# Reordering VectorE's work within a group of a Mamba-2 mixer, with finer waits

## The reference

```
proj = h @ w_in                      # z, x, B, C, dt
xBC  = silu(causal_conv4(xBC))       # depthwise, 4 taps
# 8 groups, each with its own B, C (128 states) and 4 heads of 64
a_cum = cumsum(dt * A) within a chunk of 128 positions
y_diag = ((C B^T) * exp(a_cum_q - a_cum_s), causal) @ (x dt)        # within a chunk
states = B^T (exp(a_end - a_cum) x dt), carried over the 4 chunks
y_off  = exp(a_cum) * (C @ carried state)                          # inter-chunk part
y = y_diag + y_off + x * d_skip
y = rmsnorm_per_group(y * silu(z)) * norm_g ;  out = y @ w_out
# samples: h_new = exp(dt A) h_old + dt B x^T ;  y = C h_new  (h: 8 x 32 x 64 x 128)
```

## Time and profile before

| | us |
|---|---|
| median of 3 runs | 1680.85 (1678.82 to 1683.0) |
| profiled execution | 1682.01 |
| its span, first to last instruction | 1680.3 |

### The profile page before, as it was taken

How to read it: one execution, slowest core, us unless ns; L and a number is a source line. 1 busy time by engine, 2 the same in 40 slices (tenths; PEclk the granted TensorE clock), 3 DMA queues, 4 the chain that set the end, 5 groups by cost and what they waited for, 6 DMA issues and landing times.

```text
span 1680.3 us, 30210 instructions
## 1 busy us (share of the span) xinstructions
PE 1571.3 (94%) x12653; PEld 1545.7 (92%) x12653; DVE 909.1 (54%) x1020; ACT 618.4 (37%) x827; POOL 374.0 (22%) x431
## 2 busy tenths in 40 slices
PE   6898878979987899999999999999999999999996
PEld 5898877879886799999999999999999999999996
DVE  3477688772876785343444453464455535344353
ACT  5656646622665242121212343342233212122221
POOL 1067576650665730000000022200001000000001
PEclk9999898989998999999999999999999999999998
DMA  5354445343544332332232332222223232233221
GB/s 151 93 158 127 138 129 164 118 133 94 147 125 136 107 104 81 96 101 91 85 100 76 101 114 89 76 77 89 89 76 101 76 101 89 89 99 98 78 76 51
DMA packets 158910, 173.19 MB, mean 103 GB/s; under 512 B 13912, under 2 KB 146896, under 8 KB 158784
## 3 DMA queue, kind: packets, MB, share of 16 engines
q1 hardware_dynamic: 137032, 131.30, 25.6%
q0 software_dynamic: 9472, 26.50, 5.6%
q10 hardware_dynamic: 12288, 13.71, 2.8%
HBM read 159.53 MB, written 12.21 MB: 102 GB/s over the span
## 4 chain that ended last, share of the span: by engine, by line
PE 63%; DVE 1%; ACT 1%; issue 0%; POOL 0%; ACTq 0%; DVEq 0%
PE ps L510 61%; PE ps L859 1%; PE ps L530 1%; PE ps L827 0%; PE ps L774 0%; PE ps L553 0%; DVE w_lo L1551 0%; PE ps L625 0%; POOL ssum L1415 0%; ACT arena L1359 0%; ACT w_hi L914 0%; PE ps L899 0%; PE ps L851 0%; POOL arena L1483 0%; DVE work L1557 0%
## 5 line engine op out<-in xcount | busy, mean ns | idle before, releaser
L510 PE MATMUL ps<-h_hi,w_hi 128*128 128x260 f32 (+2 forms) x2320 | 482.0, 289 | 5.2 <-issue 4.6
L510 PE MATMUL ps<-h_lo,w_hi 128*128 128x260 f32 (+2 forms) x2320 | 472.0, 285 | 0.0
L510 PE MATMUL ps<-h_hi,w_lo 128*128 128x260 f32 (+2 forms) x2320 | 471.9, 285 | 0.0
L1551 DVE TENSOR_TENSOR w_lo<-w,w_hi 128x2048 fp32r<-128x2048 f32 (+2 forms) x122 | 280.3, 2298 | 183.2 <-ACT w_hi L914 183.2
L510 PEld LDWEIGHTS ps<-h_hi,w_hi 128*128 128x128 f32 x2320 | 365.4, 192 | 7.8 <-issue 5.8
L510 PEld LDWEIGHTS ps<-h_lo,w_hi 128*128 128x128 f32 x2320 | 363.5, 191 | 0.0
L510 PEld LDWEIGHTS ps<-h_hi,w_lo 128*128 128x128 f32 x2320 | 363.2, 191 | 0.0
L914 ACT ACTIVATE w_hi<-w 128x2048 fp32r<-128x2048 f32 (+2 forms) x122 | 229.3, 1879 | 326.9 <-PE ps L510 326.7
L510 PE MATMUL ps<-a_hi,w_hi 128*128 128x260 f32 x1504 | 307.2, 286 | 9.2 <-DVE a_lo L1642 5.3
L510 PE MATMUL ps<-a_hi,w_lo 128*128 128x260 f32 x1504 | 305.5, 285 | 0.0
L510 PE MATMUL ps<-a_lo,w_hi 128*128 128x260 f32 x1504 | 305.0, 285 | 0.0
(11 more groups left out here) (208 smaller groups left out, 1370.4 us busy)
## 6 DMA issues: line engine op xcount, KB each, us to landing
w<-in_mlp_w_up SPq DMA_DIRECT2D x32, 1024.0 KB, 5.7
w<-in_mlp_w_down SPq DMA_DIRECT2D x32, 1024.0 KB, 5.2
w<-in_ssd_w_in SPq DMA_DIRECT2D x16, 1024.0 KB, 6.4
w<-in_cm_w_in SPq DMA_DIRECT2D x16, 1024.0 KB, 5.7
w<-in_ssd_w_in SPq DMA_DIRECT2D x16, 512.0 KB, 6.6
arena<-in_state_ssm POOLq DMA_DIRECT2D x64, 128.0 KB, 3.8
arena<-scr_a ACTq DMA_DIRECT2D x16, 512.0 KB, 3.9
arena<-scr_bc POOLq DMA_DIRECT2D x32, 256.0 KB, 3.9
```

Of the source, the lines that this page charges most:

```text
L510: mm = pe.matmul(ps[:, 2 * slot + b, 0:tn], w[:, pair.slot, k, col:col + P], x[:, k, t0:t0 + tn], start=(k == 0 and n == 0), stop=(k == ti ...
L1551: nc.vector.tensor_tensor(w_lo[:, pair.slot, k, w], w32[:, pair.slot, k, w], w_hi[:, pair.slot, k, w].bitcast(F32), ALU.subtract).then_inc ...
```

## The change

Nothing is computed otherwise; VectorE's list is reordered, three waits of other engines are bound to earlier marks, and the semaphore `cchain` now counts the decay products of the inter-chunk part only.

- `combine` is cut in two. The new `combine` does the product with the decay for both tiles and then adds it into `work` (new semaphore `yadd_done`). The new `gate` does the two 8-column sample operations (new `ysmp_done`), which wait for sample 3, and then the gate products.
- VectorE's order behind `y_diag(g,0)` and the first convolution becomes: `xdt` scaling, `y_diag(g,1)`, second convolution, `split_w`, sample 0, `states`, third convolution, sample 1, `combine`, fourth convolution, samples 2 and 3, `gate`.
- In window 7: `xdt` scaling, `y_diag(g,1)`, `evac_out(1)`, `split_w`, sample 0, `evac_out(2)`, `states`, sample 1, `evac_out(3)`, `combine`, samples 2 and 3, `gate`. Before, sample 0 stood ahead of `evac_out(0)` there.
- TensorE's `state_out` and the wait ahead of it ask for `cchain` in place of `comb_done`; ScalarE's `abc_load(g,0)` asks for `yadd_done`.

```diff
@@ -631,7 +633,7 @@
                 pe.wait_ge(hstep_done, 4 * g + 4)
-                pe.wait_ge(comb_done, 2 * g + 1)
+                pe.wait_ge(cchain, 2 * g + 1)
@@ -652,7 +654,7 @@
                 if due(2 * g - 1):
-                    pe.wait_ge(comb_done, 2 * g - 1)
+                    pe.wait_ge(cchain, 2 * g - 1)
@@ -1114,7 +1116,7 @@
                     if due(2 * g):
-                        act_e.wait_ge(comb_done, 2 * g)
+                        act_e.wait_ge(yadd_done, 2 * g)
@@ -1697,21 +1699,26 @@
             def combine(g):
 
                 for i in range(2):
-                    n = 3 * (2 * g + i)
                     dve.wait_ge(yoff_done, 2 * g + i + 1)
                     dve.wait_ge(ef_done, 2 * g + i + 1)
                     nc.vector.tensor_tensor(abc[:, 0, i, CH:TP], ps[:, 5 + i, CH:TP], abc[:, 0, i, CH:TP], ALU.mult)\
                       .then_inc(cchain, 1)
-                    if i == 0:
-                        dve.wait_ge(sred_done, 4 * g + 4)
+                for i in range(2):
+                    dve.wait_ge(cchain, 2 * g + i + 1)
+                    dve.wait_ge(y1_done, 2 * g + i + 1)
+                    nc.vector.tensor_tensor(work[:, i, CH:TP], work[:, i, CH:TP], abc[:, 0, i, CH:TP], ALU.add)\
+                      .then_inc(yadd_done, 1)
+
+            def gate(g):
+
+                dve.wait_ge(sred_done, 4 * g + 4)
+                for i in range(2):
                     nc.vector.scalar_tensor_tensor(out=work[:, i, TP:T], in0=act[:, g % 2, 2 + i, S0:CONV_N:TAPS],
                                                    scalar=dtf[:, 2 * g + i, 16:17], in1=ysmp[:, i, :],
-                                                   op0=ALU.mult, op1=ALU.add).then_inc(cchain, 1)
-                    dve.wait_ge(cchain, n + 1)
-                    dve.wait_ge(y1_done, 2 * g + i + 1)
-                    nc.vector.tensor_tensor(work[:, i, CH:TP], work[:, i, CH:TP], abc[:, 0, i, CH:TP], ALU.add)\
-                      .then_inc(cchain, 1)
-                    dve.wait_ge(cchain, n + 3)
+                                                   op0=ALU.mult, op1=ALU.add).then_inc(ysmp_done, 1)
+                for i in range(2):
+                    dve.wait_ge(ysmp_done, 2 * g + i + 1)
+                    dve.wait_ge(yadd_done, 2 * g + i + 1)
                     dve.wait_ge(evac_done, Pair(group_pair(g, 2)).unit(i, 1))
                     nc.vector.tensor_tensor(work[:, i, :], work[:, i, :], zs[:, i, :], ALU.mult)\
                       .then_inc(comb_done, 1)
@@ -1748,41 +1755,39 @@
                 split_w(Pair(group_pair(nxt, 1) if more else J_OUT1 + 1))
                 if not more:
                     y_low(g - 1)
-                    sample(g, 0)
-                if not more:
                     evac_out(0)
                 decayed(g, 1)
                 y_diag(g, 0)
                 if more:
                     conv(nxt, 0)
-                if not more:
-                    evac_out(1)
-                sample(g, 0 if more else 1)
-                split_w(Pair(group_pair(nxt, 1) + 1 if more else J_OUT1 + 2))
-                if more:
-                    conv(nxt, 1)
                 dve.wait_ge(ydiag_done, 2 * g + 2)
                 nc.vector.tensor_tensor(xdt[:, :, :].rearrange("p c (h d) -> p c h d", d=HD),
                                         xdt[:, :, :].rearrange("p c (h d) -> p c h d", d=HD),
                                         tokS[:, 1, :, 4 * g:4 * g + 4].unsqueeze(3).broadcast_to([P, NC, 4, HD]),
                                         ALU.mult).then_inc(xdte_done, 1)
                 y_diag(g, 1)
+                if more:
+                    conv(nxt, 1)
+                else:
+                    evac_out(1)
+                split_w(Pair(group_pair(nxt, 1) + 1 if more else J_OUT1 + 2))
+                sample(g, 0)
                 if not more:
                     evac_out(2)
-                if more:
-                    sample(g, 1)
-                if more:
-                    conv(nxt, 2)
                 if g == 0:
                     dve.wait_ge(cdec_landed, 16)
                 states(g)
-                sample(g, 2)
+                if more:
+                    conv(nxt, 2)
+                sample(g, 1)
                 if not more:
                     evac_out(3)
+                combine(g)
                 if more:
                     conv(nxt, 3)
+                sample(g, 2)
                 sample(g, 3)
-                combine(g)
+                gate(g)
 
 
             dve.wait_ge(par_landed, 48)
```

More of the change, by code:

```diff
@@ L337, in hybrid_step @@
         comb_done = sem("comb_done")
+        yadd_done = sem("yadd_done")
+        ysmp_done = sem("ysmp_done")
         ysq_done = sem("ysq_done")
```

## The result

The changed kernel took 1720.16 us (median of 4 runs, 1717.48 to 1723.23), the kernel before 1679.84 us beside it (4 runs, 1678.57 to 1683.0): the ratio is 1.0238, with a 95% interval of 1.0214 to 1.0261. It is slower by 40 us, where 17 were forecast. The direction was right and the time lies above the range.

The account below looks back on a forecast made before the run. The prediction took a ring through GpSimd, without TensorE, as the bound. Five regular groups +2.5, group 0 +3.1, group 3 +1.4 and group 7 +9.0 gave 16.0 us more than 1682.01: 1698, set at 1697 for the median; range 1673 to 1711.

Parts of the forecast that it names:

- The ring through GpSimd: Per-group cycle from VectorE's last gate through ScalarE, first convolution, GpSimd's states, sample 3 and combine: 59.08 us in group 2.
- C: In each group, the moment the next group's first convolution ends on VectorE; 26.94 us after the gate in group 2.
- the landing of the third state: GpSimd's third-state load in a regular group: predicted to arrive at C+14.1 against C+11.6 before, 2.5 us later.
- the upper bound of C+15.8: Latest predicted third-state landing in a regular group: C+7.7, 2.0 us of issuing, then 6.1 us of waiting.
- turns between queues: Rival for the third-state load: GpSimd waits 6 us again after a load issued 4.2 us later; 1711 us; chance 0.14.
- the predicted +3.1: Group 0's term: state landing +7.0 us, states 2 and 3 -1.9, gate -2.0; together +3.1.
- its ring was 58.2 and would be like the others, 59.6: Group 3's term, whose load had no weights beside it (3.29 us) but C came 2.5 us late: +1.4 us.
- the ring point: Where VectorE's last gate ends and the next group's split starts; 59.08 us apart across group 2.
- Five regular groups: Groups 1, 2, 4, 5 and 6: landing +2.5 and shorter combine -2.0 us give +0.5 each, +2.5 in all.
- Group 7: Last group's term: third-state landing +12.9 us, states 2 and 3 -1.9, gate -2.0; together +9.0.
- The cut of `combine`: Less VectorE work behind the last sample: the 384-column products and additions leave the ring, 2.0 us in each of 8 groups.
- The upper bound of the sum (+30): Sum with the latest landing: five times +2.2, group 0 +4.9, group 3 +3.1, group 7 +10.8 us; 1711 us.

Follow-up runs that it names:

- experiment 3: Kernel before with only combine cut in two, the gate alone last and the finer waits; sample, scaling and convolution order as before: 1668.21 us, ratio 0.9933.
- experiment 9: Kernel before with one edit on GpSimd: after each state, loads for the next are issued ahead of this one's stores: 1654.96 us, ratio 0.9841.
- experiment 1: Changed kernel with only sample 0 put back behind the first convolution, in group 7 ahead of evac_out(0): 1661.12 us, ratio 0.9891.
- experiment 2: Kernel before with only sample 0 moved late, behind xdt scaling and y_diag(g,1) (in window 7 sample 1 stays behind it): 1713.07 us, ratio 1.02.
- experiment 4: Changed kernel, with SyncE issuing a group's middle weights only once GpSimd has taken up the third state: 1696.77 us, ratio 1.0106.
- 7: experiment 6's kernel with sample 1 earlier still, ahead of the state steps, and GpSimd's loads ahead of its stores: 1651.15 us, ratio 0.9837.
- experiment 8: experiment 6's kernel with GpSimd's loads ahead of its stores and nothing else: 1650.61 us, ratio 0.9806.
- experiment 10: Changed kernel with GpSimd's loads ahead of its stores and nothing else: 1702.86 us, ratio 1.0134.
- experiment 6: experiment 1's kernel with sample 1 also a place forward, between the state steps and the third convolution: 1658.06 us, ratio 0.9872.
- experiment 5: Changed kernel with sample 0's product one place forward, just ahead of the split of the middle weights: 1685.57 us, ratio 1.0035.

## Why the prediction was right or wrong

**Right: what bounds the kernel.** The ring through GpSimd sets the time and TensorE is not in it. Two edits that leave TensorE's wait for scaling in place gained 12 us (experiment 3) and 25 us (experiment 9), and the change that removed both of TensorE's waits lost 40. What was said of the parts beside the ring held: the waits at L706 and L636 went, and TensorE's wait moved to the transposes behind SiLU, 12.8 us each where about 10 were given.

**Right: where the moved sample bites.** GpSimd resumes at C+7.7, as summed; it waits 3.73 us there (about 4 predicted) and 11.19 in group 7 (12 predicted); from sample 3 to the split 2.95 us (3.0). Putting the sample back takes the whole loss away (experiment 1), and moving it alone makes most of it (experiment 2).

**Wrong: the landing of the third state.** The step was: "In between: the weights wait for the split, are now issued at C+7.1 ... so C+14.1. I take it since the same transfers compete, with the weights further ahead." Measured: C+16.1, a little above even the upper bound of C+15.8. The step that failed is the price of the overlap: it added the 6.99 us which had passed between the issue of the weights and the landing to a later issue of the weights. But in the kernel before half of the state load was already out when the weights were issued, and now none of it is: from the weights' issue (238.81) to the state (248.05) it is 9.24 us. The wait after the issue was 6.42 us in this group and 5.9 to 6.9 in seven of eight, as it had been where weights came in among the load (6.13). With the weights held back it was 2.5 to 4.5 (experiment 4), with the weights 5.0 us ahead 2.99 (experiment 2), with them 4.8 us behind the first issue 2.95 (experiment 1). The head start of 0.8 us was too short to be worth anything. The rival "turns between queues" described this; it had a chance of 0.14 and its 1711 was also too low.

"The same transfers compete" left out ScalarE's 512 KB, whose place against the state load the change turned round. In group 7, which has no such transfer, the figure nearly held: the state was there 6.6 us after the weights' issue, where 6.9 were given, and the landing wait was 3.76 us. In the other groups it was 8.7 to 9.7 us. The weights of group 7 are also cut into larger pieces (272 packets of the hardware queue there against 1040 in group 2, for the same 1 MB), so the case doesn't separate the two. What the runs show is that the weights are 21 us of the loss when ScalarE's transfer is there (experiment 4). What ScalarE's transfer costs by itself stays open.

The Trainium skill, DMA: Bandwidth & Descriptors, section Queues, rings and completion order, says that each DMA engine goes round the queues in turns, packet by packet. By that rule a head start helps only once the large load is nearly through. The trace agrees: 6.42 us after 0.8 us of it against 6.13 with the weights among the issues, and 2.99 after 5.0 us, where the weights had landed 5.7 us after their issue.

**The same step in groups 0 and 3.** For group 0 the prediction had the state 7.0 us after the issue of the weights; it started at 122.65, 2.8 us later than that. The states 2 and 3 then took 17.3 us to 139.96 and not 15.6, for the fourth's landing wait was 3.96 us: together 4.5 of the 4.6 us that separate +7.7 from the predicted +3.1. For group 3, "its ring was 58.2 and would be like the others, 59.6" failed: in the kernel before a C that was 2.5 us late had been made good by a load without weights (3.29). Now C is late again (29.6 us after the ring point, 26.5 in group 2) and the load has weights beside it (6.86): both are paid, 64.87 us, +6.7 instead of +1.4.

**The sum again, with what was measured.** The ring points moved by 36.4 us up to the end of group 7; 16.0 were predicted. Five regular groups: 14.3 instead of 2.5, +11.8. Of this the landing is 2.0 a group, and GpSimd's pass from the third state's start to the fourth's end 0.7 (16.3 instead of 15.6). C itself was 0.4 sooner. Group 0: +4.6. Group 3: +5.3. Group 7: 7.8 instead of 9.0, -1.2. That makes 20.5 us, against 20.4 missing (the rest is rounding); 1.1 us more of the span came behind group 7. The cut of `combine`, -2.0 a group, measured 2.0 by itself in the seven groups other than group 3 (experiment 3). The upper bound of the sum (+30) fell short because it gave group 3 only +3.1 and kept the 15.6.

**Gains missed on the way.** The prediction took the ring's pieces for fixed. Experiments 1 and 9 show that they are not: weights issued behind the state load's last issue save 3 us of landing, whether the split is later (experiment 1) or the load sooner (experiment 9), and the stores that GpSimd issues ahead of its loads are 1.5 us of the ring, twice in a group.

The fastest versions, 7 and 8, are 29 to 30 us below the kernel before and 69 to 70 below the changed one. They keep all of the change but the place of samples 0 and 1, and turn GpSimd's loads and stores round.

**Open.** Why C is late in group 3 in every version was not tried. That the landing wait in experiment 4 is still 4.1 to 4.5 us in three groups, with no weights beside it, is not explained: ScalarE's transfer is 1.3 to 1.6 us ahead of the load in groups 1 to 6, but in three of them the wait is 2.8 to 3.4 us. Why loads ahead of stores brings C forward (experiment 8), and 17 us instead of 12 in experiment 10, was not followed up.

## What to carry to other kernels

When engines wait for each other in a cycle, follow one period of it and write down every buffer that is refilled in it: an operation that frees such a buffer (here 1.4 us of sample product) is as urgent as the load behind it, however small it is and however idle its result's reader is. Cover for a moved load has to be looked up at the new moment, for its own queue and for all the others, whatever engine issues them: a small load issued beside a large one is priced by the overlap, and a term from a row in which they overlapped half must not be shifted as if it were whole. Within a queue that issues both, loads that someone waits for go ahead of stores that nobody waits for.

## What the runs showed of the hardware

A state load (256 KB of `scr_bc` and two transfers of 128 KB, issued by GpSimd in 2.0 us) left GpSimd waiting 2.7 to 3.0 us when neither weights nor `scr_a` were issued within 4 us of its first issue (experiment 1). With 1 MB of weights among the issues it was 5.9 to 6.1 us (the kernel before, five groups). With the weights 0.8 us ahead and ScalarE's 512 KB 0.4 to 1.6 us ahead it was 5.9 to 6.9 (the changed kernel, groups 0 to 6), and 3.76 in group 7, without ScalarE's. Weights issued 0.6 us behind the last issue cost nothing when ScalarE's transfer came after the landing (experiment 9, 4.9 us from first issue to state). With that transfer 0.6 us behind the first issue and the weights 0.7 us behind the last, it was 6.5 us (experiment 5).

VectorE's and GpSimd's instructions on tiles in SBUF took longer when they ran side by side: three convolution steps took 3.49 us beside GpSimd's arithmetic and 2.42 without, GpSimd's 256-column product 0.92 beside them and 0.61 without (experiment 6). Through this a wait removed from the ring can come back as longer instructions. The Trainium skill, SBUF — State Buffer, section SBUF: two separate sides, describes a port pair of the two engines that is held for a whole instruction and blocks the other. The trace agrees that they collide: here GpSimd's product grew by 0.3 us and three of VectorE's steps by 1.1 in all.
